# A three-block transformer kernel on one Trainium2 core: GpSimd instead of VectorE makes the low halves of 132 weight units

## The reference

```python
def first_block(...):
    for l in range(DEPTH):                      # 2
        h = rms_norm(x, norm_gain[l])
        # l = 0: h @ w_in_a, dilated window attention in 3 groups of 8 heads
        # l = 1: h @ w_in_b, gated linear recurrence (hgrn2_mixer), 8 heads
        # both: cross attention to mem through w_mem_kv[l], 4 heads
        y = jnp.concatenate([mix, mem_out], axis=-1) * jax.nn.silu(gate)
        x = x + y @ w_out

def second_block(...):
    for i in range(DEPTH_2):                    # 4: gla, mla, conv, gla
        x = layer_norm(ALPHA * x + h, ln_g[i, 0], ln_b[i, 0])
        x = layer_norm(ALPHA * x + sq_relu_mlp(x, mlp_w1[i], mlp_w2[i]), ln_g[i, 1], ln_b[i, 1])
        x = x + jax.nn.sigmoid(x @ ple_w_gate[i]) * (p[i] @ ple_w_proj[i])
```

## Time and profile before

| what | value |
|---|---|
| median of 3 runs | 1888.64 us (1884.83 to 1889.47) |
| the profiled execution's own time | 1887.82 us |
| its span, first to last instruction | 1886.0 us |
| PE busy | 1850.3 us, 98% of the span |
| DVE busy | 1145.3 us, 61% |
| ACT busy | 934.6 us, 50% |
| POOL busy | 577.6 us, 31% |
| mean granted TensorE clock | 0.996 |

### The profile page before, as it was taken

How to read it: one execution, slowest core, us unless ns; L and a number is a source line. 1 busy time by engine, 2 the same in 40 slices (tenths; PEclk the granted TensorE clock), 3 DMA queues, 4 the chain that set the end, 5 groups by cost and what they waited for, 6 DMA issues and landing times.

```text
span 1886.0 us, 25520 instructions
## 1 busy us (share of the span) xinstructions
PE 1850.3 (98%) x10144; PEld 1600.0 (85%) x10144; DVE 1145.3 (61%) x2026; ACT 934.6 (50%) x1092; POOL 577.6 (31%) x128
## 2 busy tenths in 40 slices
PE   7999999999999999999999999999999999999998
PEld 5888888888898988888888888899888889888887
DVE  5788878877888788222776422576622287862227
ACT  5655555445654554444554544453444455544443
POOL 0000000000000002888201788400588800058880
PEclk9999999999999999999999999999999999999999
DMA  8344444554243334655443555454655543365551
GB/s 311 137 158 155 146 163 155 185 195 149 97 157 118 133 134 184 223 178 194 178 178 134 192 189 200 179 200 155 233 198 185 197 179 134 107 234 201 188 194 65
DMA packets 53562, 325.02 MB, mean 172 GB/s; under 512 B 8625, under 2 KB 12081, under 8 KB 16209
## 3 DMA queue, kind: packets, MB, share of 16 engines
q1 hardware_dynamic: 45200, 309.97, 45.4%
q10 hardware_dynamic: 8256, 13.58, 2.2%
HBM read 322.48 MB, written 1.05 MB: 172 GB/s over the span
## 4 chain that ended last, share of the span: by engine, by line
PE 86%; DVE 9%; issue 2%; ACT 1%; SPq 1%; DMA 0%; DVEq 0%; ACTq 0%
PE project L1032 32%; PE output L1032 30%; PE turn L1404 5%; PE project L1404 5%; PE project L1410 2%; PE turn L1410 2%; PE turn L1232 2%; DVE wlo L1846 2%; PE output L1195 1%; PE output L1172 1%; DVE arena L2187 1%; SPq L961 1%; DVE arena L1964 1%; DVE arena L2210 1%; PE turn L1151 1%
## 5 line engine op out<-in xcount | busy, mean ns | idle before, releaser
L998 POOL TENSOR_TENSOR wlo<-raw,whi 128x2048 fp32r<-128x2048 f32 x124 | 577.4, 4689 | 1259.8 <-ACT whi L1473 1243.1
L1473 ACT ACTIVATE whi<-raw 128x2048 fp32r<-128x2048 f32 x291 | 550.6, 1910 | 327.6 <-PE project L1404 166.1
L1032 PE MATMUL project<-whi,XT 128*128 128x512 f32 x1376 | 450.9, 398 | 1.9 <-DVE arena L1997 0.9
L1846 DVE TENSOR_TENSOR wlo<-raw,whi 128x2048 fp32r<-128x2048 f32 x167 | 379.6, 2285 | 21.9 <-ACT whi L1473 21.6
L1032 PEld LDWEIGHTS project<-whi,XT 128*128 128x128 f32 x1376 | 258.5, 188 | 56.1 <-DVE wlo L1846 1.9
L1032 PE MATMUL output<-whi,YTh 128*128 128x512 f32 x736 | 288.8, 392 | 1.5 <-DVE YTl L2339 1.5
L1032 PE MATMUL output<-whi,YTl 128*128 128x512 f32 x736 | 287.3, 390 | 0.0
L1032 PE MATMUL output<-wlo,YTh 128*128 128x512 f32 x736 | 287.0, 390 | 0.0
L2623 DVE TENSOR_TENSOR arena<-project,arena 128x256 f32<-128x256 f32 x48 | 20.4, 425 | 409.0 <-ACT arena L1802 409.0
L1032 PE MATMUL project<-wlo,XT 128*128 128x512 f32 x688 | 268.0, 390 | 0.0
L1032 PE MATMUL project<-XT,whi 128*128 128x256 f32 x1184 | 219.0, 285 | 0.0
(11 more groups left out here) (270 smaller groups left out, 2394.1 us busy)
## 6 DMA issues: line engine op xcount, KB each, us to landing
raw<-in_units SPq DMA_DIRECT2D x291, 1024.0 KB, 4.8
arena<-in_ln_g ACTq DMA_DIRECT2D x8, 512.0 KB, 5.3
arena<-in_ln_b ACTq DMA_DIRECT2D x8, 512.0 KB, 6.8
tok<-in_mem SPq DMA_DIRECT2D x2, 512.0 KB, 6.1
arena<-in_mem_norm_gain ACTq DMA_DIRECT2D x2, 512.0 KB, 5.1
xres<-in_x SPq DMA_DIRECT2D x1, 1024.0 KB, 13.2
arena<-in_mem ACTq DMA_DIRECT2D x1, 1024.0 KB, 6.5
arena<-in_p ACTq DMA_DIRECT2D x4, 256.0 KB, 3.4
```

The costliest lines, as they stand in the source:

```text
L998: pool.tensor_tensor(wlo[:, slot, :], raw[:, slot, :], whi[:, slot, :], ALU.subtract).then_inc(lo_pool, 1)
L1032: mm = pe.matmul(out, x if x_stationary else w, w if x_stationary else x, start=start and i == 0, stop=stop and i == 2, skip_group_check=True)
L1473: act.activation(whi[:, slot, :], raw[:, slot, :], ACT.Copy).then_inc(hi_done, 1)
L1846: dve.tensor_tensor(wlo[:, slot, :], raw[:, slot, :], whi[:, slot, :], ALU.subtract).then_inc(lo_dve, 1)
```

## The change

From unit 6 on, POOL and not DVE makes the low halves of the units of eleven named matrices: the input and output projections of all layers and the memory keys and values. These are 132 units. With the MLP's 124, POOL now has 256 of 291. DVE keeps units 0 to 5, the last MLP unit of each layer, the `ple_w_gate` and `ple_w_proj` units, and the five small units of the latent attention. POOL takes its units in the order of the ring, between the four MLP loops. Nothing else in the lists changes; the `less` that TensorE's MLP loop subtracts now counts the new division.

```diff
+POOL_MATRICES = ("w_in_a", "w_out_a", "w_mem_kv", "w_in_b", "w_out_b", "gla_w_in", "gla_w_out", "mla_w_in", "mla_w_out", "conv_w_in", "conv_w_out")
+POOL_FROM = 6
...
-        on_pool = [u[0] == "mlp1" or u[0] == "mlp2" and u[2:] != (1, FF_CHUNKS - 1) for u in units]
+        on_pool = [m >= POOL_FROM and isinstance(u[0], tuple) and u[0][0] in POOL_MATRICES or
+                   u[0] == "mlp1" or u[0] == "mlp2" and u[2:] != (1, FF_CHUNKS - 1) for m, u in enumerate(units)]
...
+            def stretch(begin, end):
+
+                for m in range(begin, end):
+                    if on_pool[m]:
+                        lo(m, m % RING)
+
+            done = 0
             for first, normed in ((f["n"], f["src_n"]) for kind, f in steps if kind == "mlp"):
+                stretch(done, first)
                 for s in range(RING):
...
+                done = first + 4 * FF_CHUNKS
...
+            stretch(done, NU)
...
-                    less = n0 - (4 * FF_CHUNKS - 1) * f["i"] - 1
+                    less = n0 - sum(on_pool[:n0]) - 1
```

## The result

The changed kernel takes 2176.02 us (median of five runs, 2174.24 to 2176.58) against 1885.56 us for the kernel before on the same chip: ratio 1.1535, 95% interval [1.1523, 1.1548]. It is 15% slower. The profiled execution's span is 2173.8 us, against 1886.0.

What follows compares the result with a forecast made beforehand. It took TensorE's issue of matmuls as the bound, DVE second with hardly any slack in places. Terms 84 + 28 + 28 + 4.5 + 10 = 154.5 on the profiled 1887.8 gave about 2042, stated as 2040 us, range 1930 to 2130.

Steps and rivals of the forecast that it cites:

- A DVE operation with two inputs in SBUF and a POOL subtraction exclude each other.: Wherever both run: each waits for the other's whole instruction, up to 4.62 us of DVE for each 2.28 saved.
- Three blocks, 13.9 us ... the transpose stands 12 us late: K's post in a group: POOL gets in three times, 13.9 us, and PE's transpose is 12 us late.
- two blocks ... 7 us late, 19 us: Q's post in a group: two blocks, 9.2 us, the copy 7 us late; with K's, 19 us a group.
- I take 14 us a group: Six attention groups, units 6 to 41: 14 us each (bounds 5 and 19), 84 us in all (30 to 114).
- The other stretches, by the sum of times without DVE's waits: 306 to 435 us: +28; four level stretches: +28; convolution: +4.5; the other 42 moved units: 10.
- TensorE's clock falls too: Rival: PE's new waits bring the lower clock to some 700 us of slowed stretches, another 84 us, 2125 at full price.
- beyond 2130: Whole kernel: lower clock, 84 us, plus level and output stretches keeping their waits, 21 and 22 us; chance 0.08.
- One block per chain: Rival for DVE's chains: DVE, once in, keeps POOL out to the chain's end; 6 us a group, about 1960; chance 0.22.
- faster: Rival: POOL's time falls on PSUM work, reduces and DVE's waits; DVE gains, at best 1876 us; chance 0.07.
- small loss: Rival: blocks lie in slack and only a few slots are late; 10 to 30 us, 1900 to 1920; chance 0.05.
- the bound of 13 us on a gain: Most a lighter DVE can return: PE's waits for it, about 13 us over twelve lines of the wait list.
- POOL keeps up: In the group a unit comes every 6.9 us and POOL needs 4.62, so low halves are ready in time.

Runs made afterwards that it cites:

- run 7: Changed kernel with only units 6 to 47 on POOL, each low half waiting for the Q or K posts formerly ahead of it on DVE: 1915.92 us.
- Runs 8 and 9: Kernel before, unused DVE reductions repeated behind layer 0's rotary K and Q group scales: 20 and 13 times, 2033.74 us; 7 and 4 times, 1939.25 us.
- run 5: Changed kernel with only units 6 to 47 moved to POOL, the other 90 back on DVE: 2017.88 us.
- run 4: Changed kernel with each of POOL's moved low halves made in four instructions of 512 columns: 2121.58 us.
- run 1: Changed kernel with POOL subtracting only 64 of 2048 columns in the 132 moved units, the other columns left stale: 1880.63 us.
- run 2: Changed kernel with POOL only writing zeros over the low halves of the 132 moved units, reading nothing: 1878.33 us.
- Run 6: Changed kernel with only units 66 to 99 and 240 to 253 moved to POOL: 1990.12 us.

## Why the prediction failed

The mechanism, its sign and its place were right, the time was not: 2040 (1930 to 2130) against 2176. By its own steps:

**"A DVE operation with two inputs in SBUF and a POOL subtraction exclude each other."** Right: L1876 and L1883 go from 0.17 to 4.55 and 4.58 us at most, while L2140, with an input in PSUM, keeps to 277 to 425 ns. One kind of operation was missing from it: `negm`, with one input in SBUF, is blocked too (2.86 us in the changed kernel, 4.47 in run 7). And "here every DVE operation is a two-input one" was too strong for the levels: the selected copies out of PSUM (L2253, the old L2240) kept to 0.75 us. The rule of the Trainium skill (SBUF — State Buffer, "Who interferes with whom"), under which the second to come waits for the whole instruction, agrees with the trace: 4.42 to 4.55 us for a 0.17 us operation, beside three subtractions of 13.55 us in all. That POOL comes in again after each small operation is what the timelines here show. Two lines of the changed kernel:

```profile
L1876 DVE TENSOR_TENSOR st<-st x48: 160/166/4553, 24.0 to 1928.7; 128x8 f32<-128x8 f32 x40, 128x2 f32<-128x2 f32 x6, 128x4 f32<-128x4 f32 x2
...
L2140 DVE CUSTOM_DVE_ANT_0 arena<-output,arena x80: 277/418/425, 87.5 to 1251.1; 128x256 f32<-128x256 f32 x48, 128x128 f32<-128x128 f32 x32
```

**"Three blocks, 13.9 us ... the transpose stands 12 us late", "two blocks ... 7 us late, 19 us".** The blocks were right to a few tenths: the changed kernel has three subtractions in K's chain (13.55 us) and two in Q's (9.16). PE's waits were 11.4 us for 12 and 4.5 for 7, 16 in all. The group lost 19.9, near the 19 by luck: the count put 3 us too much on the waits and nothing on the clock, which cost 3.8.

**"I take 14 us a group"** is the first step that failed. Next to a count of 19, followed through the timeline step by step, I set a sum of busy times (46.4 to 55.3 us a group) and took the lower one because "a late PE also holds ACT, and with it POOL". A sum of busy times was no ceiling there. DVE's waits did not shrink when its work grew; they doubled. In a group of 61.2 us DVE was busy for 41.58, less than the 46.4 of the sum, and idle for 19.6 where it was idle for 8.95, and the trace puts 18 of the 19.6 down to waits for PE's outputs, as PE waited for DVE. These six groups lost 116.5 us where 84 stood.

**"The other stretches, by the sum of times without DVE's waits"** failed by the same step, and by more. Units 42 to 61: +44.3 for 28 (with DVE's waits kept, 49, it would have been near). The levels and the output projections beside them, 46 units: 74.5 + 29.5 = 104, where I had 28 for the 21 units of four level stretches and a part of the 10 for the other 25. The full price of a block above a low half, 2.34 us, would have given 46 x 2.34 = 108. The reasons, "they have fewer chains with PE right behind them" and that blocks would fall "into DVE's free time", don't fit the rows: in units 66 to 95 DVE was blocked for 103 us, and its idle time went from 38.7 up to 78.8. The convolution was nearly right (6.5 for 4.5).

**"TensorE's clock falls too"** was a rival with 84 us, kept out of the sum; that is the third term that failed. PE's busy time rose by 83.9 us, at granted clocks of 0.87 to 0.92 in the four slow stretches. That the figure fits is partly luck: the share was 10% of 736 us of matmuls there, for an assumed 12% of 700. Its mistake was to be a separate case. Runs 8 and 9 show that it is a part of the main mechanism, 3.7 us in a group in which PE waited for 4 us or longer, and 5.9 in run 5. With it and with the waits of the levels and outputs kept, as the prediction's case "beyond 2130" had them, its own terms come to 2042 + 84 + 21 + 22 = 2169, against 2176; that case had a chance of 0.08.

**The rivals.** "One block per chain" fell with the timeline of the group and with run 4, "faster" and "small loss" with the result; the bound of 13 us on a gain was generous (6 us in run 1, 8 in run 2). "POOL keeps up" was right: PE waited for `wlo` no more than before (1.9 us for 2.1). Of the signs named ahead, one did not come: POOL's median stayed (4618 ns for 4622), though its longest rose from 5305 to 5967.

**What stays open.** The level stretches were not followed operation by operation. Run 6 shows that their loss comes from POOL's low halves there, and the rows show 103 us of blocks in units 66 to 95; how these blocks became 74.5 us was not traced. Of the 104 us of both level stretches, 37.7 are longer matmul time (242.5 to 270.4 and 117.2 to 127.0). Why like waits cost 3.8 us of matmul time in one kernel and 5.9 in another is open as well: PE worked at the lower level for some 7 us of the group in the changed kernel and for some 12 us of it in run 5. A cheaper placement of POOL's low halves was not looked for; runs 1 and 2, with hardly a block, gained 6 and 8 us.

## What to carry to other kernels

Before moving work to GpSimd, look up in the trace whether DVE runs chains of small dependent SBUF operations beside it: each pending GpSimd instruction that reads SBUF gets in between two of them and can cost up to its own length, here 4.6 us for each 2.3 us saved. Where two engines hand work to and fro, follow one period step by step and trust that count above a sum of busy times, which leaves out that each waits for the other. And add to a new wait of PE the matmuls behind it, which ran at the lower clock for some microseconds.

## What the runs showed of the hardware

- A GpSimd write of 1.81 us doesn't hold up DVE's small operations with two SBUF inputs (169 ns at most). A GpSimd subtraction of 1.85 us does (up to 1.78 us), and 132 of them cost the kernel 47 us. The one-input `TENSOR_SCALAR` waits for either: up to 1.79 us beside the write, 4.47 beside the 4.62 us subtraction.
- DVE and GpSimd alternate one instruction at a time: twelve subtractions of 1.27 us held up twelve successive DVE operations, eight of them independent of each other.
- Behind a wait of PE of 3.9 us the granted clock was 0.50 (1.2 GHz) over 5 us with PE busy throughout, then 0.98, and the group had 3.7 us more of matmul time. A wait of 0.8 us in the same group left the clock at 1.00. Two waits of 12.6 and 7.3 us in a group cost 3.7 us together, two of 9.5 and 4.5 us in run 5 cost 5.9.
- The changed kernel's mean granted clock is 0.941 against 0.996; by the two levels that is an estimate of 256 and 15 us at the lower one (2 x 0.059 x 2173.8 and 2 x 0.004 x 1886).
